# A last output projection computed by halves of the tokens, the first half inside the rows of the last head

## The reference

```python
# layer b, 8 heads; o is (tokens, 8 x 128)
w = p[:, :, 0] - lam * p[:, :, 1]          # two softmaxes, block-causal mask
o = einsum(w, v)                           # per head
o = rmsnorm(o per head) * (1 - LAMBDA_INIT) * silu(gate)
y = o @ w_out_b                            # 1024 x 1024
x = x + rmsnorm(y, post_norm)              # the output
```

## Time and profile before

| | us |
|---|---|
| runs of the kernel | 2897.41, 2900.5, 2902.43; median 2900.5 |
| profiled execution, first to last instruction | 2898.2 |
| PE busy | 2763.6 (95%) |
| VectorE busy | 1600.6 (55%) |
| ScalarE busy | 684.3 (24%) |
| mean granted clock of PE | 0.987 of full speed |

### The profile page before, as it was taken

How to read it: one execution, slowest core, us unless ns; L and a number is a source line. 1 busy time by engine, 2 the same in 40 slices (tenths; PEclk the granted TensorE clock), 3 DMA queues, 4 the chain that set the end, 5 groups by cost and what they waited for, 6 DMA issues and landing times.

```text
span 2898.2 us, 35623 instructions
## 1 busy us (share of the span) xinstructions
PE 2763.6 (95%) x13514; PEld 2207.5 (76%) x13530; DVE 1600.6 (55%) x1982; ACT 684.3 (24%) x1246; POOL 305.4 (11%) x303
## 2 busy tenths in 40 slices
PE   8989988999999999999999999999999999999996
PEld 6756656778888888877888888888767778777774
DVE  7755563545555445564554544454466666666654
ACT  2233341211111111131011011011033433344431
POOL 0699800000000000001000000000000000000000
PEclk9999999999999999999999999999999999999998
DMA  4211112234344333424222222221233222222131
GB/s 168 87 59 59 61 55 102 87 116 159 132 159 145 143 147 116 164 96 157 76 72 87 78 81 72 87 82 63 87 143 119 75 82 76 74 74 72 55 123 66
DMA packets 48634, 286.61 MB, mean 99 GB/s; under 512 B 6592, under 2 KB 6720, under 8 KB 18624
## 3 DMA queue, kind: packets, MB, share of 16 engines
q1 hardware_dynamic: 21776, 118.50, 11.7%
q0 software_dynamic: 14544, 105.91, 10.7%
q10 hardware_dynamic: 12256, 61.39, 5.5%
HBM read 248.03 MB, written 29.36 MB: 96 GB/s over the span
## 4 chain that ended last, share of the span: by engine, by line
PE 84%; DVE 10%; ACT 3%; issue 3%; DMA 1%; DVEq 0%; SPq 0%; ACTq 0%
PE PB L240 12%; PE PB L242 12%; PE PB L241 12%; PE OBB L240 9%; PE OBB L241 9%; PE OBB L242 9%; PE TBB L772 4%; PE TBB L240 2%; PE TBB L242 2%; PE TBB L241 2%; PE PB L821 2%; PE OBB L886 2%; PE PB L827 1%; PE OBB L881 1%; DVE on L2052 1%
## 5 line engine op out<-in xcount | busy, mean ns | idle before, releaser
L240 PE MATMUL PB<-HH,WH 128*128 128x512 f32 x1488 | 588.7, 396 | 26.2 <-DVE A L549 8.9
L241 PE MATMUL PB<-HL,WH 128*128 128x512 f32 x1488 | 583.3, 392 | 0.0
L242 PE MATMUL PB<-HH,WL 128*128 128x512 f32 x1488 | 583.1, 392 | 0.0
L240 PE MATMUL OBB<-HH,WH 128*128 128x512 f32 x1024 | 416.4, 407 | 16.1 <-ACT vF L1008 7.5
L241 PE MATMUL OBB<-HL,WH 128*128 128x512 f32 x1024 | 401.3, 392 | 0.0
L242 PE MATMUL OBB<-HH,WL 128*128 128x512 f32 x1024 | 400.6, 391 | 0.0
L240 PEld LDWEIGHTS PB<-HH,WH 128*128 128x128 f32 x1488 | 282.2, 190 | 92.8 <-issue 29.7
L241 PEld LDWEIGHTS PB<-HL,WH 128*128 128x128 f32 x1488 | 282.3, 190 | 60.8 <-issue 2.2
L242 PEld LDWEIGHTS PB<-HH,WL 128*128 128x128 f32 x1488 | 281.7, 189 | 59.5
L256 DVE TENSOR_TENSOR WL<-RAW,WH 128x2048 fp32r<-128x2048 f32 x101 | 234.8, 2325 | 53.4 <-DMA WH<-units 42.1
L2292 POOL DMA_DIRECT2D WH<-units x85 | 45.5, 536 | 1934.6 <-PE PB L240 1172.3
(11 more groups left out here) (345 smaller groups left out, 4001.7 us busy)
## 6 DMA issues: line engine op xcount, KB each, us to landing
RAW<-units SPq DMA_DIRECT2D x85, 1024.0 KB, 4.7
WH<-units POOLq DMA_DIRECT2D x85, 1024.0 KB, 5.0
gs<-units ACTq DMA_DIRECT2D x16, 1024.0 KB, 4.8
gu<-gs ACTq DMA_DIRECT2D x16, 1024.0 KB, 3.9
RAW<-gu SPq DMA_DIRECT2D x16, 1024.0 KB, 4.9
WH<-gu POOLq DMA_DIRECT2D x16, 1024.0 KB, 5.9
tmpd<-xr SPq DMA_DIRECT2D x112, 64.0 KB, 2.0
A<-xT SPq DMA_DIRECT2D x4, 1024.0 KB, 10.2
```

Of the source, the lines that this page charges most:

```text
L240: first = pe.e.matmul(out, wh, xh, start=start, stop=False)
L241: pe.e.matmul(out, wh, xl, start=False, stop=False)
L242: return pe.e.matmul(out, wl, xh, start=False, stop=stop), first
```

## The change

The last projection is computed by halves of the tokens. The norm of the heads' output and the gate are split too: rows 0 to 3 give tokens 0 to 511. Their norm (`scaled(0)`), transposes, gate and split are done inside rows 4 and 5 of the last head; the silu of the gate moves to row 3. Output tiles 0 to 5 for the first half of tokens are computed in rows 6 and 7 and after row 7, each complete over all eight channel tiles; tiles 6 and 7 follow when the heads' second half has been transposed. Then all eight tiles for the second half of the tokens run in the order 4, 5, 6, 7, 0, 1, 2, 3, and units 0 and 1 are loaded a second time as `U_WOB + 4` and `U_WOB + 5`. The first half's total, root, normalisation, addition and store are interleaved with the second half's products. The quarters (`part_pe`) and `whole_pe` are gone from this head; rows 1 to 5 have the two warming products. All eviction of products goes to ScalarE. SP issues the stores, in eight pieces, and `x` comes back in ten.

```diff
-NU = U_WOB + 4
+NU = U_WOB + 6
@@ turn in attend_pe
-                if not more and not forget and not c and t in PART_ROWS[False]:
-                    part_pe(pe, t, False)
-                elif not more and t and not c and not (forget and t in PART_ROWS[True]):
+                if not more and t and not c and not (forget and t in PART_ROWS[True]) and not (late and t > 5):
                     warm(pe, TB[0], 1 if forget else 2)
@@ rows in attend_pe
             for t in range(NB):
                 projections(t)
+                if late:
+                    late(t, 0)
                 if t:
                     values(t - 1)
+                if late:
+                    late(t, 1)
...
             projections(NB)
+            if late:
+                late(NB, 0)
             values(NB - 1)
+            if late:
+                late(NB, 1)
+                return
@@ rows in attend_act
                 halves_out(t)
-                if t and more and True:
+                if late:
+                    late(t, 0)
+                if t and (more or late):
                     row_out(t - 1)
+                if t and late:
+                    block_out(t - 1)
+                if late:
+                    late(t, 1)
@@ new
+        LAST_ROWS = {6: (0, 1), 7: (2, 3), 8: (4, 5)}
+        LAST_ORDER = (4, 5, 6, 7, 0, 1, 2, 3)
+        LAST_UNITS = (U_WOB + 2, U_WOB + 3, U_WOB + 4, U_WOB + 5)
...
+        def out_half_pe(pe, bank, n, m, h, name):
+            for k in range(KT):
+                c = m % 2 * 1024 + k * P
+                mm, first = mm3(pe, bank, WH[n % 2][:, c:c + P], WL[n % 2][:, c:c + P], HH[:, k, cols_of(h)],
+                                HL[:, k, cols_of(h)], k == 0, k == KT - 1)
...
+        def early_out_pe(pe, m):
+            if m % 2 == 0:
+                unit(pe, U_WOB + m // 2)
+            if m == 6:
+                pe.fresh = False
+            if m == 0:
+                pe.e.wait_ge(dve_done, at_mark(pe, "dve", "lo7_0"))
+            elif m < 6:
+                pe.e.wait_ge(act_done, at_mark(pe, "act", f"f{m - 1}"))
+            out_half_pe(pe, early_bank(m), U_WOB + m // 2, m, 0, f"f{m}")
+
+        def last_pe(pe, t, place):
+            if t == 5 and place == 0:
+                pe.e.wait_ge(dve_done, at_mark(pe, "dve", "on0"))
+                transposes(pe, DB, lambda b: ot[:, b, :], range(4), "ot0")
+            if t in LAST_ROWS:
+                early_out_pe(pe, LAST_ROWS[t][place])
+            if t == NB and place == 1:
+                pe.e.wait_ge(dve_done, at_mark(pe, "dve", "on1"))
+                transposes(pe, TB[0], lambda b: ot[:, b, :], range(4, NB), "ot1")
+                for m in (6, 7):
+                    early_out_pe(pe, m)
...
+        def last_act(act, t, place):
...
+            if t == 3 and place == 0:
+                e.wait_ge(dve_done, at_mark(act, "dve", "rawg1"))
+                e.activation(sg[:, :], sg[:, :], ACT.Silu).then_inc(act_done, act.mark("silu"))
+                e.preload_act_table_set(LN_EXP)
+            if t == 5 and place == 1:
+                high(0)
+            if t in LAST_ROWS:
+                if place == 0:
+                    out(LAST_ROWS[t][0])
+                else:
+                    a, b = LAST_ROWS[t]
+                    last_square_act(act, a, a, 0)
+                    out(b)
+                    last_square_act(act, b, b, 0)
+            if t == NB and place == 1:
+                high(1)
+                for m in (6, 7):
+                    out(m)
+                    last_square_act(act, m, m, 0)
+
+        def last_dve(dve, t, place):
...
+            if (t, place) == (4, 1):
+                scaled(0)
+            elif (t, place) == (5, 0):
+                gated(0)
+            elif (t, place) == (5, 1):
+                low(0)
+            elif (t, place) == (6, 1):
+                low_part(dve, U_WOB + 1)
+            elif (t, place) == (7, 1):
+                last_sum_dve(dve, 1, 0)
+                low_part(dve, U_WOB + 2)
+            elif t == NB:
+                last_sum_dve(dve, 2, 0)
+                last_sum_dve(dve, 3, 0)
+                scaled(1)
+                low_part(dve, U_WOB + 3)
+                gated(1)
+                last_sum_dve(dve, 4, 0)
+                low(1)
+                for j in (5, 6, 7):
+                    last_sum_dve(dve, j, 0)
...
+        def last_out_pe(pe, ph):
+            pe.start(ph, "diff_last")
+            pe.tiles_of = None
+            pe.e.wait_ge(dve_done, done_in("dve", "diff_last", "lo7_1"))
+            for j, m in enumerate(LAST_ORDER):
+                n = LAST_UNITS[j // 2]
+                if j >= 4 and j % 2 == 0:
+                    unit(pe, n)
+                elif j == 2:
+                    pe.fresh = True
+                if j == 3:
+                    pe.e.wait_ge(act_done, done_in("act", "diff_last", "f7"))
+                if j == 7:
+                    pe.e.wait_ge(act_done, at_mark(pe, "act", f"y{LAST_ORDER[0]}"))
+                out_half_pe(pe, LAST_BANKS[j], n, m, 1, f"d{m}")
+                if j == 1:
+                    last_total_pe(pe, 0, TB[0])
+            warm(pe, OBB, 3)
+            last_total_pe(pe, 1, TB[1])
+
+        def last_out_dve(dve, ph):
...
+            last_sum_dve(dve, 1, 1)
+            for k in range(3):
+                tile(k, 0)
+            low_part(dve, U_WOB + 4)
+            last_sum_dve(dve, 2, 1)
+            for k in (3, 4):
+                tile(k, 0)
+            last_sum_dve(dve, 3, 1)
+            tile(5, 0)
+            last_sum_dve(dve, 4, 1)
+            low_part(dve, U_WOB + 5)
+            tile(6, 0)
+            last_sum_dve(dve, 5, 1)
+            tile(7, 0)
+            for j in (6, 7):
+                last_sum_dve(dve, j, 1)
+            for k in range(KT):
+                tile(k, 1)
@@ SP's queue, behind the last units
+            for h in range(2):
+                for n in range(4):
+                    sp.wait_ge(dve_done, at_mark(steps, "dve", f"add{2 * n + 1}_{h}"))
+                    sp.dma_start(io["out"].rearrange("(k p) s -> p k s", p=P)[:, 2 * n:2 * n + 2, cols_of(h)],
+                                 A[:, 2 * n:2 * n + 2, cols_of(h)]).then_inc(stored, 16)
@@ layout of the weights
+    units[U_WOB + 4:NU] = units[U_WOB:U_WOB + 2]
```

More of the change, by code:

```diff
@@ L154, in build @@
         x_again = [sem(f"x_again{n}") for n in range(4)]
+        x_last = [[sem(f"x_last{h}{n}") for n in range(4)] for h in range(2)]
         stored = sem("stored")
@@ L803, in square_sums, with attend_pe @@
                 pe_done, pe.mark(f"n{x}{h}"))
-        def attend_pe(pe, i, forget, plan, u0, more, fill=None):
+        def attend_pe(pe, i, forget, plan, u0, more, fill=None, late=None):
             last_evac = [None]
@@ L945, in attend_pe @@
             if forget and not more:
-                part_pe(pe, NB, True)
+                part_pe(pe, NB)
+            if late:
+                late(NB, 0)
             values(NB - 1)
+            if late:
+                late(NB, 1)
+                return
             if not forget:
                 projections(NB + 1)
-            if not more and not forget:
-                for k in (4, 5):
-                    whole_pe(pe, U_WOB, k, k == 4)
             pe.e.wait_ge(dve_done, at_mark(pe, "dve", f"r{NB - 1}b" if forget else "on", i))
@@ L1009, in value_half_act, with attend_act @@
                 act_done, act.mark(f"rawv{h}"))
-        def attend_act(act, i, forget, plan, more, block_out=None, early=(), fill=None):
+        def attend_act(act, i, forget, plan, more, block_out=None, early=(), fill=None, late=None):
             e = act.e
@@ L1085, in attend_act @@
                     exps(t + 1, 1)
-                if not (more and True):
+                if not (more or late):
                     row_out(t)
-                    if block_out and t + 1 < NB:
-                        block_out(t)
-                elif block_out and t:
+                elif block_out and t and not late:
                     block_out(t - 1)
+            if late:
+                late(NB, 0)
+                row_out(NB - 1)
+                block_out(NB - 1)
+                late(NB, 1)
+                return
             if not forget:
@@ L1106, in attend_act, with attend_dve @@
                 row_out(NB - 1)
-        def attend_dve(dve, i, forget, plan, u0, more, early=(), fill=None):
+        def attend_dve(dve, i, forget, plan, u0, more, early=(), fill=None, late=None):
             e = dve.e
@@ new lines, in last_total_pe @@
+        def last_total_pe(pe, h, bank):
+            pe.e.wait_ge(dve_done, at_mark(pe, "dve", "acc7_1") if h else done_in("dve", "diff_last", "acc7_0"))
+            pe.e.matmul(bank, ones[:, :], sqe[h][:, 0, :], start=True, stop=True).then_inc(
+                pe_done, pe.mark(f"total{h}"))
+        def last_out_pe(pe, ph):
[17 more added lines that the diff above has]
+            last_total_pe(pe, 1, TB[1])
@@ L2177, in block_out @@
```

(11 more changed lines are left out.)

158 lines of the change are left out of this document (113 added, 45 removed).

## The result

| | before | after |
|---|---|---|
| median of the runs, us | 2900.59 (2897.41 to 2902.43, 4 runs) | 2916.06 (2914.16 to 2917.55, 4 runs) |
| profiled execution, us | 2898.2 | 2915.9 |

The change makes the kernel 15.5 us slower: ratio 1.005, 95% interval 1.0039 to 1.0062. Forecast were 14.0 us slower and 2914.5.

What follows compares the result with a forecast made beforehand. TensorE bounds the kernel until its last product, then VectorE carries the tail. Four waits (23.8 us), slow clock (8.4) and the other terms put the last product 28.2 later; the tail gives 14.2 back: 14.0 slower, 2914.5, range 2904 to 2923.

Steps and rivals of the forecast that it cites:

- T4 of row 4 earlier: Row 4, last head: without the quarter that held them, the transposes of row 4 go 3.3 us earlier.
- wait for `on0`: Row 5, before values 4 and T5: TensorE idles 6.3 us for a VectorE product queued behind weights 5.
- wait for `lo7_0`: Before the first early half: TensorE idles 5.7 us for a low part that VectorE does after weights 6.
- wait for split `U_WOB+1`: Row 7, before half 2: TensorE idles 7.8 us for a split that stands behind weights 7.
- wait for split `U_WOB+2`: Before half 4: TensorE idles 4.0 us for a split behind T7's two evictions and one square sum.
- half clock behind the four: After each of the four waits TensorE runs slow, losing 2.1 us each, 8.4 in all.
- late units in the second half: Second half's products: the reloaded unit `U_WOB+4` costs between 0 and 2.5 us once; taken as 0.
- end behind the last product: Tail after the last product: 18.5 us in total, against 32.7 before, so 14.2 back.
- TensorE's work: Whole projection: TensorE's amount of work is unchanged, 384 products, so the end of the products moves by the waits alone.
- One sign that was to show the prediction wrong: After a wait: products of 0.23 us right away would show the prediction wrong.
- Rival (a): Rows 4 to 7: waits as forecast but the clock stays high, 5.6 us slower, 2906; chance 0.10.
- Rival (b): Early halves hide under the rows' loop, none of the four waits exists: 18 us faster, 2882; chance 0.09.
- Rival (c): Clock stays slow through rows 4 to 6 and a unit is late twice: up to 10 more, 2925; chance 0.15.

Runs made afterwards that it cites:

- experiment 1: Changed kernel with VectorE splitting the two weight units before it takes out the transposes of rows 6 and 7: 2901.7 us, 14.4 less than the changed kernel.
- 2: Changed kernel with the first early half's wait for channel tile 7 put right before tile 7's products: 2909.18 us, 6.9 less than the changed kernel.
- experiment 5: Changed kernel with splits, tile wait and early scaling all moved, plus the first half's tile 7 low part before row 6's maxima: 2886.64 us.
- experiment 3: Changed kernel with the scaling of the first four output blocks ahead of row 5's maxima on VectorE: 2911.83 us, 4.2 less than the changed kernel.
- experiment 4: Changed kernel with its four waits left in place and mostly filled with warming products on constants: 2910.15 us, 5.9 less than the changed kernel.
- experiments 7: Changed kernel with VectorE normalising the first half's eight tiles only after the second half's last square sum: 2924.73 us, 8.7 more than the changed kernel.
- 6: Kernel of experiment 5 with SP sending the first half's stores only once the last weight unit is split: 2886.92 us.

## Why the prediction was right

The direction, the mechanism and the size held: 15.5 slower where 14.0 was forecast, inside the range. That the four waits and the clock are the cause is shown by removing them (experiment 1 two of them, 2 and 3 one each), by filling them (4), and by removing all together (5). Point by point:

| step | forecast | measured |
|---|---|---|
| T4 of row 4 earlier | 3.3 | 3.2 (28.7 from row 1's warming before, 25.5 after) |
| wait for `on0` | 6.3 | 6.24 |
| wait for `lo7_0` | 5.7 | 5.72 |
| wait for split `U_WOB+1` | 7.8 | 7.74 |
| wait for split `U_WOB+2` | 4.0 | 3.75 |
| half clock behind the four | 8.4 | about 7.1 by the windows (0.50 x 3.9, 0.50 x 4.1, 0.48 x 3.4 and 0.34 x 4.4); 6.8 by filling the waits |
| late units in the second half | 0 | 1.1 |
| last product later | 28.2 | 28.7 |
| end behind the last product | 18.5 | 19.8 |
| net | 14.0 | 15.5 |

That the last product is only 0.5 off is in part luck: the clock was put 1.3 too high and the late unit 1.1 too low.

**TensorE's work.** The prediction says that the end of the products moves by the waits alone. Its sum is better than that sentence: it has 1.7 for the two warming products of row 5, which stand behind the stop for `on0` and ahead of T5. In the changed kernel they hold T5 up by 2.15 (2770.16 to 2772.31), though the weights were done at 2766.5. In the count they are offset by the short stops of rows 5 to 7 before the change (1.31, 0.37 and 0.51), which are gone. No run leaves these warming products out by themselves.

**The clock.** The term was 1.3 too large, as I priced each burst near the middle of what the old trace showed. One sign that was to show the prediction wrong, products of 0.23 right after a wait, did appear behind the fourth stop, for about 1.3 us before the clock fell; the idea that each burst starts slow holds for three of the four. Rival (a), that the clock would hold, is refuted by experiment 4: it would have made filling the waits worth nothing. The pairs of warming products in rows 4 and 5 did not keep the clock up across the stop that followed them.

**The loads.** I gave a late unit between 0 and 2.5 and took 0, and the unit that I named was in time, if barely: in experiment 3 PE stops 0.25 for it. The one after it was late, and for another reason: I had looked at the reload of `x`, and what collided was the stores of the first half, whose issue the overlap had moved beside the last two weight loads.

**The tail.** I took a pair of 512 columns at 1.3; the eight pairs take 11.5 (2901.11 to 2912.58), 1.43 each. The two forms take 0.75 and 0.69 and overlap hardly at all: each addition starts 0.03 to 0.10 after its product has ended, each next product 0.08 before the addition ends. That is 1.1 of the 1.3 by which the tail was missed. The bound by the durations (1.4) was the right one, and the old rows already said so: the prediction reads a pace of 2.45 out of them, but 20.0 for eight pairs is 2.50, nearly the sum of 1.28 and 1.23.

**Rival (b)**, that the early halves hide under the rows' loop, was not true of the change as written. But experiment 5 lands where (b) would: 2886.6 against its 2882. The premise was sound that the rows have room, and what decided was only where VectorE's four operations and one wait of TensorE stood. My reason against it, that the weights can't come earlier, held for the weights and not for what was queued behind them. For the split of `U_WOB+2` it wasn't even the order of the kernel: that split stands behind T7's evictions and a square sum, as the prediction's own sum for the fourth wait has it.

**Rival (c)**, a clock that stays low through rows 4 to 6, did not occur: the scores of rows 5 and 6 ran at full clock. One unit was late, by 1.1, and not twice.

## What to carry to other kernels

When work is moved to fill an engine, its inputs have to move too: ask of each wait what stands ahead of it in the releasing engine's own order, and whether that has anything to do with it. Here three operations of 0.7 to 2.3 us stood behind a chain of 5 us that they did not need, and a fourth behind 2 us, with 15 us of idle VectorE ahead of two of these chains; moving the four and one wait of TensorE turned 15.5 us lost into 13.3 won. A wait for the last of several inputs belongs ahead of the use of that input, not ahead of the first. And a stop of TensorE can cost more than its length: 1.5 to 2.0 us each for the four here, and 3.0 for one of them in another trace.

## What the runs showed of the hardware that was not expected

Three stores of 512 KB and a load of 1 MB in flight made another load of 1 MB land after 8.7 to 8.9 us (changed kernel, experiment 5) instead of 5.1, and after 6.9 to 7.1 with the other load alone beside it (experiments 7 and 6). Splitting a VectorE operation of 1024 columns (1.28 and 1.23) into halves (0.75 and 0.69) costs 0.15 to 0.22 more per whole. A pair is paced at nearly the sum of its two durations at either width: 1.43 against 2.50, so halving the width made the pair 0.57 and not 0.5 as long.

The same stop is not always followed by the same clock. The stop of 7.74 in row 7 was followed by 3.4 us of half clock in the changed kernel and by 6.0 in experiment 3. Behind the fourth stop (3.75, 3.74) the products began on full clock in the changed kernel and on half clock (0.80 for the first) in experiment 3. A stop of 1.76 ahead of T5 was followed by half clock in experiment 3 and by none in experiment 5. So what one stop costs in clock is known from these traces to about 1 us, while the four together came out alike: 7.1 by the windows and 6.8 by filling them.
